# Prompt matrix memory of an mLSTM layer: one product for query and key blocks, raw-input state, the normaliser as column 513

## The reference

```python
q = headwise(xc, wq); k = headwise(xc, wk); v = headwise(xm, wv)      # blocks of 4 channels
...
sc = jnp.einsum('bqhd,bshd->bqsh', qc, kc) * wts
num = jnp.einsum('bqsh,bshd->bqhd', sc, vc) + a[..., None] * jnp.einsum('bqhk,bhvk->bqhv', qc, C)
den = jnp.sum(sc, axis=2) + a * jnp.einsum('bqhk,bhk->bqh', qc, n)
h = num / jnp.maximum(jnp.abs(den), jnp.exp(-m_t))[..., None]
...
C_new = decay[..., None, None] * C + jnp.einsum('blh,blhv,blhk->bhvk', wg, vc, kc)
n_new = decay[..., None] * n + jnp.einsum('blh,blhk->bhk', wg, kc)
```

## Time and profile before

| | us |
|---|---|
| median of 3 runs | 4144.98 (4135.86 to 4145.65) |
| the profiled execution | 4136.48 |
| its span | 4133.7 |
| busy: PE / weight loads / DVE / ACT / POOL | 3676.8 / 3268.5 / 1933.9 / 1140.2 / 484.4 |
| mean granted clock of PE | 0.937 |
| setup | 1939.7 to 1989.4 |
| streams | 1989.4 to 2328.4 |
| prompt | 2328.4 to 2896 |
| store | 2896 to 2913.9 |

### The profile page before, as it was taken

The page is one execution under the profiler, slowest core; times in us unless marked ns, Lnnn a source line. Parts: engine busy times, 40 slices in busy tenths (PEclk is TensorE's granted clock), DMA queues, the critical chain, the costliest instruction groups (busy, mean ns, idle before and its releaser), DMA issues. The chain is left out here.

```text
span 4133.7 us, 54309 instructions
## 1 busy us (share of the span) xinstructions
PE 3676.8 (89%) x20853; PEld 3268.5 (79%) x20853; DVE 1933.9 (47%) x3063; ACT 1140.2 (28%) x1862; POOL 484.4 (12%) x733
## 2 busy tenths in 40 slices
PE   5549899999999989997499699999797799999997
PEld 4449889999999979995344466666797799999996
DVE  8924444454444642223434344445466345444455
ACT  5223343323323322221132111111212332332331
POOL 2230110101001100001200211111000110000000
PEclk7669999999999999998699799999998899999998
...
DMA packets 357903, 332.07 MB, mean 80 GB/s; under 512 B 39491, under 2 KB 285443, under 8 KB 357567
## 3 DMA queue, kind: packets, MB, share of 16 engines
...
...
## 5 line engine op out<-in xcount | busy, mean ns | idle before, releaser
L1579 PE MATMUL bank<-x_head,w_head 128*128 128x384 f32 x1488 | 508.1, 341 | 69.1 <-DVE w_rest L840 41.0
L1579 PE MATMUL bank<-x_rest,w_head 128*128 128x384 f32 x1488 | 505.3, 340 | 0.0
L1579 PE MATMUL bank<-x_head,w_rest 128*128 128x384 f32 x1488 | 504.6, 339 | 0.0
L840 DVE TENSOR_TENSOR w_rest<-w_raw,w_head 128x1024 fp32r<-128x1024 f32 x228 | 281.9, 1236 | 461.6 <-ACT w_head L836 461.5
L836 ACT ACTIVATE w_head<-w_raw 128x1024 fp32r<-128x1024 f32 x228 | 242.4, 1063 | 743.6 <-PE bank L856 194.7
L1238 PE MATMUL bank<-x_head,w_head 128*128 128x384 f32 x1056 | 354.1, 335 | 8.9 <-DVE w_rest L840 7.4
L1238 PE MATMUL bank<-x_rest,w_head 128*128 128x384 f32 x1056 | 353.6, 335 | 0.0
L1238 PE MATMUL bank<-x_head,w_rest 128*128 128x384 f32 x1056 | 353.6, 335 | 0.0
L1579 PEld LDWEIGHTS bank<-x_head,w_head 128*128 128x128 f32 x1488 | 285.2, 192 | 75.2 <-issue 66.1
L1579 PEld LDWEIGHTS bank<-x_head,w_rest 128*128 128x128 f32 x1488 | 285.4, 192 | 0.0
L1579 PEld LDWEIGHTS bank<-x_rest,w_head 128*128 128x128 f32 x1488 | 285.2, 192 | 0.0
...
## 6 DMA issues: line engine op xcount, KB each, us to landing
...
f<-in_state_mlstm_C_dram SPq DMA_DIRECT2D x40, 256.0 KB, 4.3
...
```

The lines of the kernel that those rows point to most:

```text
L840: dve.tensor_tensor(self.rest[slot][:, :], self.raw[slot][:, :], self.head[slot][:, :].bitcast(F32), ALU.subtract).then_inc(self.split, 1)
L1579: m = pe.matmul(out[:, 0:TB], lhs[slot][:, P * k:P * k + P], rhs[:, k, TB * c:TB * c + TB], start=(k == 0 and q == 0), stop=(k == KD - 1 a ...
```

## The change

For the prompt alone, with the 4 by 4 blocks of one head as Wq and Wk:

- The scores are xc' (Wq Wk') xc, so the product of the blocks is made once, in the setup (`wk4`, `fold`, a fourth block-diagonal tile `bd[:, 3]`), and the queries by channels are multiplied by it; the keys' side of the scores is `xc` itself.
- The state holds values by raw `xc` instead of values by keys. Instead of keys by rows, `xc` is transposed. At the end the key blocks `bd[:, 1]` are multiplied in: 64 matmuls in place of the 64 transposes.
- `v` has a 513th column of ones, and `ct` a 513th column, which is the normaliser. Read-out and updates are 513 columns wide, over two PSUM banks (a pair), in matmuls of 256 and 257 columns. The nine one-column matmuls and the array `nt` go. The updates take turns in two pairs (`wide(n)`).
- The two rows of each step come from a DRAM copy (`rows_d`) by a broadcast DMA into `cell.row`, in the streams too. The PE matmuls that broadcast them go.
- `xc`, `xm`, `sz` and the rows have a buffer for each head, four instead of two. `PromptCell` takes the place of `Cell`, which the streams keep.
- ACT copies values; the scores of the next step are done between the second and third update; the weights before the fourth; the exponent right after the reciprocal; the gate rows in the setup before the block-diagonal tiles. `hn` goes (in place in `h`), the skip is scaled in place in `xc`.
- The store has eight buffers, and the normaliser is written in four rows.

```diff
+        w, wk4, fold = env.sb("w", [P, 3, IT, QB]), env.sb("wk4", [P, IT, QB, QB]), env.sb("fold", [P, IT, QB])
+        rows = env.sb("rows", [H, CHUNKS, 2, P])
...
+                for q in range(QB):
+                    sp.dma_start(wk4[q:P:QB, :, :, :].rearrange("p j c d -> p j (c d)"),
+                                 wk[0].rearrange("(j n) c d -> n j (c d)", j=IT)).then_inc(w_in, 16)
...
+                sp.wait_ge(sums, 2)
+                sp.wait_ge(exps, 4)
+                sp.dma_start(rows_d.rearrange("h c k t -> h (c k t)"), rows[:, :, :, :].rearrange("h c k t -> h (c k t)")).then_inc(kept, 16)
...
-                dve.wait_ge(w_in, 48)
-                ts(w[:, 1, :, :], w[:, 1, :, :], float(DH) ** -0.5, None, ALU.mult).then_inc(scaled, 1)
-                dve.wait_ge(masked, 3)
-                for k in (0, 2, 1):
-                    if k == 1:
-                        dve.wait_ge(scaled, 1)
-                    tt(bd[:, k, :, :].rearrange("p j (n d) -> p j n d", d=QB), bcast(w[:, k, :, :], 2, NBK),
-                       bcast(bcast(mask[:, :], 2, QB), 1, IT), ALU.mult)
                 dve.wait_ge(picked, 1)
                 for c in range(NB):
+                    ins = dve.tensor_copy(lf[:, TB * c:TB * c + TB], bank[NB + c][0:H, 0:TB])
+                ins.then_inc(logs, 1)
+                for c in range(NB):
                     link(dve.tensor_copy(ig[:, TB * c:TB * c + TB], bank[c][0:H, 0:TB]))
-                    ins = dve.tensor_copy(lf[:, TB * c:TB * c + TB], bank[NB + c][0:H, 0:TB])
-                    if c < NB - 1:
-                        link(ins)
-                ins.then_inc(logs, 1)
+                scale = float(DH) ** -0.5
+                dve.wait_ge(w_in, 16 * (3 + QB))
+                tt(wk4[:, :, :, :], wk4[:, :, :, :], bcast(w[:, 0, :, :], 2, QB), ALU.mult).then_inc(scaled, 1)
+                ts(w[:, 1, :, :], w[:, 1, :, :], scale, None, ALU.mult).then_inc(scaled, 1)
+                dve.wait_ge(scaled, 1)
+                tt(wk4[:, :, :, 0:2], wk4[:, :, :, 0:2], wk4[:, :, :, 2:4], ALU.add).then_inc(scaled, 1)
+                dve.wait_ge(masked, 3)
+                wide = lambda k, src: tt(bd[:, k, :, :].rearrange("p j (n d) -> p j n d", d=QB), bcast(src, 2, NBK),
+                                         bcast(bcast(mask[:, :], 2, QB), 1, IT), ALU.mult)
+                wide(0, w[:, 0, :, :])
+                dve.wait_ge(scaled, 3)
+                tt(fold[:, :, :], wk4[:, :, :, 0], wk4[:, :, :, 1], ALU.add).then_inc(scaled, 1)
+                wide(2, w[:, 2, :, :])
+                dve.wait_ge(scaled, 4)
+                ts(fold[:, :, :], fold[:, :, :], scale, None, ALU.mult).then_inc(scaled, 1)
+                wide(1, w[:, 1, :, :])
+                dve.wait_ge(scaled, 5)
+                wide(3, fold[:, :, :])
...
+class PromptCell:
+    def __init__(self, env, bd):
+        self.bd = bd
+        two = lambda n, shape: [env.sb(f"{n}{k}", shape) for k in range(2)]
+        four_ = lambda n, shape: [env.sb(f"{n}{k}", shape) for k in range(HEADS)]
+        self.xc, self.xm, self.sz = (four_(n, [P, HT, P]) for n in ("p_xc", "p_xm", "p_sz"))
+        self.row = four_("p_row", [P, 2 * P])
+        self.q, self.qa, self.kw = (two(n, [P, HT, P]) for n in ("p_q", "p_qa", "p_kw"))
+        self.v = two("p_v", [P, DH + 1])
+        self.e, self.em, self.sc = (two(n, [P, P]) for n in ("p_e", "p_em", "p_sc"))
+        self.h, self.t1 = (two(n, [P, HT, P]) for n in ("p_h", "p_t1"))
+        self.stats, self.mv, self.small = two("p_stats", [P, 6]), two("p_mv", [P, 2]), two("p_small", [P, 4])
+    def project(self, pe, env, h, y):
+        bank, bd = env.bank, self.bd
+        for t in range(HT):
+            pe.matmul(bank[0][:, P * t:P * t + P], bd[:, 3, HT * h + t, :], self.xc[h][:, t, :], start=True, stop=True)
+        for t in range(HT):
+            pe.transpose(bank[1][:, P * t:P * t + P], self.xc[h][:, t, :], env.ident[:, :])
+        for t in range(HT):
+            ins = pe.matmul(bank[2][:, P * t:P * t + P], self.xm[h][:, t, :], bd[:, 2, HT * h + t, :], start=True, stop=True)
+        return ins
...
+                    src = rows_d[h, c] if isinstance(c, int) else rows_d[h, bass.ds(c, 1)].rearrange("o k t -> (o k) t")
+                    sp.dma_start(cell.row[h][:, :], src.rearrange("k t -> (k t)").partition_broadcast(P)).then_inc(x_in[h], 16)
...
-                    ge(pe, den_read, c, h)
-                    ge(pe, n_done, c, h)
-                    held(pe, pe_held)
-                    src = rows[:, c, :, :] if isinstance(c, int) else rows[:, bass.ds(c, 1), :, :].rearrange("h o k t -> h (o k) t")
-                    pe.matmul(bank[4][:, 0:2 * P], env.sel[:, h, :], src.rearrange("h k t -> h (k t)"),
-                              start=True, stop=True).then_inc(spread, 1)
-
                 def scores(c, h):
                     y = h % 2
-                    ge(pe, d_bank4, c, h, 1, 1)
+                    ge(pe, qk, c, h, 1, 1)
+                    ge(pe, weighted, c, h)
                     for t in range(HT):
-                        ins = pe.matmul(bank[4][:, 256:256 + P], cell.k[y][:, t, :], cell.q[y][:, t, :], start=(t == 0), stop=(t == HT - 1))
+                        ins = pe.matmul(bank[3][:, 0:P], cell.xc[h][:, t, :], cell.q[y][:, t, :], start=(t == 0), stop=(t == HT - 1))
...
-                    pe.matmul(bank[4][:, 400:401], cell.sc[y][:, :], env.ones[:, 0:1], start=True, stop=False)
-                    for t in range(HT):
-                        pe.matmul(bank[4][:, 400:401], cell.qa[y][:, t, :], nt[:, h, t:t + 1], start=False, stop=(t == HT - 1))
-                    for t in range(HT):
-                        ins = pe.matmul(bank[4][:, 404 + t:405 + t], cell.kw[y][:, t, :], env.ones[:, 0:1], start=True, stop=True)
-                    ins.then_inc(dened, 1)
+                    ge(pe, aqd, c, h, 1, 1)
+                    ge(pe, vcopied, c, h, 1, 1)
                     ge(pe, updated, c, h, HT, -1)
                     ge(pe, updated, c, h, HT, -(HEADS - 1) * HT)
-                    pe.matmul(num[:, :], cell.sc[y][:, :], flat(cell.v[y]), start=True, stop=False)
-                    for t in range(HT):
-                        ins = pe.matmul(num[:, :], cell.qa[y][:, t, :], ct[h][:, t, :], start=False, stop=(t == HT - 1))
+                    for t in range(-1, HT):
+                        for k in range(2):
+                            if t < 0:
+                                pe.matmul(half(n, k), cell.sc[y][:, :], cut_half(cell.v[y], k), start=True, stop=False)
+                            else:
+                                ins = pe.matmul(half(n, k), cell.qa[y][:, t, :], cut_half(ct[h][:, t, :], k), start=False, stop=(t == HT - 1))
                     ins.then_inc(numbered, 1)
                     nxt = after(c, h)
                     if nxt:
                         project(*nxt)
+                    ge(pe, kwd, c, h, 1, 1)
                     for t in range(HT):
                         if t == 0:
                             ge(pe, updated, c, h, HT)
                         elif t == 1:
-                            ge(pe, joined, c, h)
-                        elif t == 2:
                             ge(pe, rowed, c, h, 1, 1)
                         else:
-                            ge(pe, updated, c, h, HT, 1)
-                        pe.matmul(upd[t][:, :], cell.kw[y][:, t, :], flat(cell.v[y]), start=True, stop=True).then_inc(stat, 1)
+                            ge(pe, updated, c, h, HT, t - 1)
+                        for k in range(2):
+                            ins = pe.matmul(half(n + 1 + t, k), cell.kw[y][:, t, :], cut_half(cell.v[y], k), start=True, stop=True)
+                        ins.then_inc(stat, 1)
+                        if nxt and t == 1:
+                            scores(*nxt)
+                    ge(pe, normed, c, h, 1, 1)
                     if nxt:
-                        scores(*nxt)
-                    ge(pe, updated, c, h, HT, 2)
-                    ge(pe, normed, c, h, 1, 1)
+                        ge(pe, aqd, c, h, 1, 2)
                     for t in range(HT):
-                        ins = pe.transpose(turn[:, P * t:P * t + P], cell.hn[y][:, t, :], env.ident[:, :])
+                        ins = pe.transpose(turn[:, P * t:P * t + P], cell.h[y][:, t, :], env.ident[:, :])
...
-                    ge(act, projected, c, h, 1, 1)
-                    act.activation(flat(cell.q[y]), bank[0][:, :], ACT.Copy)
-                    act.activation(flat(cell.k[y]), bank[1][:, :], ACT.Copy).then_inc(qk, 1)
                     ge(act, exp_in, c, h, 1, 1)
                     act.activation(cell.e[y][:, :], cell.e[y][:, :], ACT.Exp).then_inc(exped, 1)
+                    ge(act, projected, c, h, 1, 1)
+                    ge(act, scored, c, h, 1, -1)
+                    ge(act, aqd, c, h, 1, -1)
+                    act.activation(flat(cell.q[y]), bank[0][:, :], ACT.Copy).then_inc(qk, 1)
```

(55 more changed lines are left out.)

160 lines of the change are left out of this document (80 added, 80 removed).

## The result

The changed kernel takes 3982.91 us (3977.46 to 3988.94), the kernel before 4142.26 (4135.86 to 4145.65): a ratio of 0.9618, 95% interval 0.9607 to 0.963. The forecast was 3985 in 3955 to 4035. The profiled execution of after took 3980.57 us, its span 3978.9, against 4136.5 and 4133.7 of before.

The account below looks back on a forecast made before the run. PE was taken to bound the prompt loop. Loop -168, setup +6, streams +2 and store +8 summed to -152 us, taken off the profiled 4136.5: 3985 us, range 3955 to 4035.

Parts of the forecast that it names:

- loop and lead-in: Prompt memory loop and its first step: 163.4 us saved over 31 steps, 4.5 in the lead-in, -168 together.
- The step: One prompt loop step: from 17.27 us to 12.0, with 11.84 of PE work at full clock.
- Handovers: PE's waits for DVE in a loop step, 0.25 us before update 2, about 0.05 more; 0.1 added net.
- The clock: PE's granted clock in the loop: 0.99 instead of 0.96, as load waits and one-column matmuls go; 0.1 us a step.
- Setup: Before the streams: fourth block-diagonal build +2.2 us, rows' store at the end 2 to 4; +6 (3 to 16).
- Streams: Streams stage: SP issues four row broadcasts, 0.5 us each, ahead of the first inputs; +2 (0 to 4).
- Store: Store of the state: 64 matmuls replace 64 transposes, PE becomes the bound; +8 us (5 to 21).
- Handover bound: Loop updates' two-pair ring, not PE, sets the step; DVE updates doubled give 13.5 us, 4031 total; chance 0.12.
- Halves dear: Read-out and update halves cost 0.31 us a record: step 15.3 us, 4087 total; chance 0.05.
- Rows late: Loop's row broadcast loads land late; landing at 30 us costs 1.3 a step, 4025 total; chance 0.03.
- Slower by the clock: PE falls to 1.2 GHz in the loop from shorter records and more transposes: 23.2 us a step, 4332; chance 0.03.
- The rule that stood against the change: Four more transposes a loop step don't count as busy, so low clock stays: step 12.35 us, 3996 total.

Follow-up runs that it names:

- a_ones: Changed kernel with eight one-column matmuls (16 records) put back before each read-out, their result unused: 4047.84 us, ratio 0.9783.
- b_both: Kernel before with four load buffers instead of two and eight of a step's nine one-column matmuls left out: 4034.01 us, ratio 0.9746.
- a_512: Changed kernel with read-out and updates as one 512-column matmul instead of two halves, normaliser column left out: 3979.45 us, ratio 0.9609.
- a_order: Changed kernel with DVE's normalisation moved behind the second state update, the weights behind it: 3969.99 us, ratio 0.9591.
- b_split: Kernel before with four load buffers and the normaliser's eight one-column matmuls moved behind the read-out, nothing left out: 4086.56 us, ratio 0.9864.
- b_no_ones: Kernel before, two load buffers kept, with eight of a step's nine one-column matmuls left out: 4172.12 us, ratio 1.0078.
- b_four: Kernel before with four load buffers instead of two, taking the load wait away alone: 4130.68 us, ratio 0.9987.
- a_mended: Changed kernel with two DMA orders changed: stores of m ahead of the rows' store, first streams loads ahead of row broadcasts: 3977.45 us, ratio 0.9612.

## Why the prediction was right, point by point

The sum was -152, the two spans differ by -155. Part of that closeness is luck, since the misses have opposite signs: loop and lead-in gave 7 us more than forecast, the streams 4 less in this pair of traces. So is the starting point: the sum was taken off the profiled execution, 4136.5. Taken off the median of the three runs known then, 4144.98, it would have given 3993, also inside the range.

- **What bounds the loop.** PE, as said: busy 362.9 of 366.0.
- **The step.** Forecast 11.84 of work, 0.1 of handovers, 0.1 of clock: 12.0. Measured 11.67 written out, 11.81 as a mean. Of the work, q and k came out as said (1.78 to 0.89) and so did the one-column matmuls (a_ones, b_both). Keys came out better: 1.88 for keys and values became 0.43 + 0.90, -0.55 for -0.45. The turn went from 0.62 to 0.44: the forecast saw a wait in it and left it in the sum, to set it against the new waits. The halves cost 0.05 (a_512) where 0.1 stood, and the line from 128 to 512 columns gave 0.217 a record, which the read-out shows (4.34 for 20).
- **Handovers.** The forecast had 0.25 ahead of update 2, some 0.05 more, and 0.2 of the old step's waits against them: 0.1 net. Measured are 0.21 ahead of update 2 and 0.09 within the second pair of updates (1.83, where a_order has 1.74), against the turn's 0.18: 0.12 net. The term was right, and a_order shows the waits as real: reordered, they go.
- **The clock.** 0.99 forecast, 1.00 measured. The direction was right, and the reason given, waits for loads and one-column matmuls, half right. b_split shows the one-column matmuls at work by themselves. The load waits of before (0.9 to 2.1 us) left the clock at 1.00; only the longer ones of b_no_ones (2.7 to 3.6 us) were followed by a low one. What the forecast didn't see is that load wait and low clock replace each other from step to step. It priced the wait as a term (0.76 a step) and the clock as another (some 0.6, in the change to 0.99), and without the wait alone b_four gained 7 us of the 24 that the wait had.
- **Registers.** Nothing stood in the sum for the hardware loop's 0.16 a step on PE, +4.2 us. Steps at 11.67 throughout would have been -174.
- **The loop and lead-in together:** -168 forecast, -175 measured.
- **Setup.** +6 forecast, +5.9 measured, partly by compensation. Reckoned from the start of the setup, the addition behind the builds starts 1.1 us later than before instead of 2.2: the four new weight loads were there when the six copies ended at 1950.2, and copies and small operations, which overlap each other in part, took 1 us less than was added up. The stores at the end took some 5, not 2 to 4. The timeline of after's setup, answering to the earlier trace rows:

```profile
1948.62 1.16 ACT L2398 ACTIVATE t<-lf 4x1152 f32<-4x1152 f32 x1 [34.90 <-DVE lf L2417]
...
1960.00 0.74 DVE L2441 TENSOR_SCALAR t<-t 4x1152 f32<-4x1152 f32 x1
```

- **Streams.** +2 (0 to 4) forecast, +6.4 measured: the one term outside its bounds in this pair of traces. By the means of several traces it is some +4 (see a_mended), at their upper end. The step that was mis-sized is "SP issues four row broadcasts, 0.5 each". They took 4.09 us, and the first projection stands 10.2 us behind the stage's start instead of 5.5. a_mended shows the place.
- **Store.** +8 forecast with 16.2 of PE and more for its tail; +6.5 measured, and 2.3 in the last step ahead of it, which had no term (a clock of 0.85 there, where that stretch of before had 0.99). The two together are 8.8.

```profile
2735.61 16.16 PE L2814 MATMUL pair<-bd,f 128*128 128x128 f32 x128 [3.16 <-PEq L2600]
...
2759.19 0.93 SPq L826 DMA_DIRECT2D w_raw<-in_mlstm_w_down_dram  x2
```

- **The rivals.** *Handover bound*: DVE's updates are 743 ns with their 513 columns in the mean, where before had 744 with 512, so not doubled. *Halves dear*: 0.217 and not 0.31. *Rows late*: 4.0 us to landing in the median of the loop, no load wait in it. DMA issues of the loop, KB each and median us to landing:

```profile
p_sz<-sz_d SPq DMA_DIRECT2D x29, 256.0 KB, 3.7
p_row<-rows_d SPq DMA_DIRECT2D x29, 128.0 KB, 4.0
```

- *Slower by the clock*: the loop stood at 1.00. The rule that stood against the change, that transposes don't count as busy for the clock gate (the Trainium skill, TensorE: Matmul & The Clock Gate, Part 4: PE-mode transpose), made no difference here: eight transposes a step lie among 60 other records, and no stretch of low clock followed. A loop of transposes alone was not run.
